# An expert's output in two rounded parts: the scatter product in one-pass form

## The reference

```
logits = x @ w_router                            # 256 x 8
top_logit, top_e = top_k(logits, 2)
gate = softmax(top_logit)
for each expert e, for the tokens routed to it:  # width 1024, hidden 3584
    y = (silu(x @ w_gate[e]) * (x @ w_up[e])) @ w_down[e]
    out[token] += gate[token, e] * y[token]
x = layer_norm(ALPHA * x + out)
```

## Time and profile before

| | |
|---|---|
| median of 3 runs | 1530.47 us (1529.55 to 1532.50) |
| profiled execution, first to last instruction | 1529.7 us |
| mean granted TensorE clock | 0.988 of full |
| TensorE busy (matmul) | 1478.0 us, 97% |
| VectorE busy | 1133.1 us, 74% |
| ScalarE busy | 966.3 us, 63% |
| read from memory | 427.87 MB |

### The profile page before, as it was taken

One profiled execution on the slowest core, in us unless ns is written; L12 is line 12 of the kernel. 1 busy time (PEld: TensorE's weight loads), 2 busy tenths in 40 slices (PEclk: granted clock), 3 DMA queues, 4 the chain that ended last, 5 costly groups with the idle time before them and its releaser, 6 DMA issues.

```text
span 1529.7 us, 20973 instructions
## 1 busy us (share of the span) xinstructions
PE 1478.0 (97%) x8040; PEld 1264.5 (83%) x8040; DVE 1133.1 (74%) x935; ACT 966.3 (63%) x910; POOL 6.2 (0%) x15
## 2 busy tenths in 40 slices
PE   8988999999988999999999999999999999999995
PEld 8987999989977788888888878888888888887883
DVE  4636444454546688888888888888888888888885
ACT  4644443355545677677677767767767767766774
POOL 1000000000000000000000000000000000000000
PEclk9999999999999999999999999999999999999998
DMA  9414555535044899799889889989989988998931
GB/s 369 148 63 167 191 186 179 189 136 185 37 193 184 323 376 377 308 369 371 340 339 373 344 334 379 369 302 375 378 322 355 370 340 337 375 371 309 377 137 57
DMA packets 59586, 429.63 MB, mean 281 GB/s; under 512 B 6720, under 2 KB 6736, under 8 KB 7568
## 3 DMA queue, kind: packets, MB, share of 16 engines
q1 hardware_dynamic: 58464, 423.65, 72.4%
q0 software_dynamic: 928, 5.02, 1.0%
q10 hardware_dynamic: 144, 0.27, 0.1%
HBM read 427.87 MB, written 1.05 MB: 280 GB/s over the span
## 4 chain that ended last, share of the span: by engine, by line
PE 91%; ACT 4%; DVE 3%; issue 1%; DMA 1%; SPq 0%; DVEq 0%; ACTq 0%
PE ps L397 27%; PE ps L399 27%; PE ps L398 27%; PE ps L684 2%; PE ps L671 2%; PE ps L693 2%; PE ps L404 1%; DVE wlo L1014 1%; ACT raw L822 1%; DMA raw<-w_dense 1%; DVE raw L1042 1%; PE ps L493 1%; ACT whi L760 1%; ACT biasb L796 1%; PE ps L549 1%
## 5 line engine op out<-in xcount | busy, mean ns | idle before, releaser
L1014 DVE TENSOR_TENSOR wlo<-raw,whi 128x2048 fp32r<-128x2048 f32 x402 | 920.8, 2291 | 242.3 <-ACT whi L760 242.0
L760 ACT ACTIVATE whi<-raw 128x2048 fp32r<-128x2048 f32 x402 | 770.4, 1918 | 313.3 <-PE ps L399 309.1
L397 PE MATMUL ps<-whi,xth 128*128 128x512 f32 (+1 forms) x1080 | 423.1, 392 | 7.5 <-ACT xth L775 6.5
L399 PE MATMUL ps<-whi,xtl 128*128 128x512 f32 (+1 forms) x1080 | 410.9, 380 | 0.0
L398 PE MATMUL ps<-wlo,xth 128*128 128x512 f32 (+1 forms) x1080 | 410.2, 380 | 0.0
L397 PEld LDWEIGHTS ps<-whi,xth 128*128 128x128 f32 x1080 | 204.3, 189 | 50.1 <-ACT xth L775 7.3
L398 PEld LDWEIGHTS ps<-wlo,xth 128*128 128x128 f32 x1080 | 204.5, 189 | 40.1 <-issue 3.8
L399 PEld LDWEIGHTS ps<-whi,xtl 128*128 128x128 f32 x1080 | 204.1, 189 | 39.5
L397 PE MATMUL ps<-whi,hth 128*128 128x512 f32 x528 | 206.4, 391 | 0.0
L399 PE MATMUL ps<-whi,htl 128*128 128x512 f32 x528 | 205.6, 389 | 0.0
L398 PE MATMUL ps<-wlo,hth 128*128 128x512 f32 x528 | 205.6, 389 | 0.0
(11 more groups left out here) (201 smaller groups left out, 800.5 us busy)
## 6 DMA issues: line engine op xcount, KB each, us to landing
raw<-w_moe SPq DMA_DIRECT2D x339, 1024.0 KB, 4.8
raw<-w_dense SPq DMA_DIRECT2D x63, 1024.0 KB, 4.8
raw<-vec_rows POOLq DMA_DIRECT2D x4, 1024.0 KB, 6.0
x<-x_in SPq DMA_DIRECT2D x2, 512.0 KB, 5.5
out<-x SPq DMA_DIRECT2D x2, 512.0 KB, 2.8
work<-bias_cst POOLq DMA_DIRECT2D x1, 576.0 KB, 8.7
con<-cst ACTq DMA_DIRECT2D x1, 262.0 KB, 4.7
work<-lam_rows POOLq DMA_DIRECT2D x1, 96.0 KB, 7.9
```

The costliest lines, as they stand in the source:

```text
L397: mm(o, lh, rh, start=start, stop=False)
L399: return mm(o, ll, rh, start=False, stop=stop)
L760: A(unit(whi, j), raw[:, slot * UNIT:(slot + 1) * UNIT], ACT.Copy).then_inc(hi_rdy, 1)
L1014: dve.tensor_tensor(unit(wlo, j), raw[:, slot * UNIT:(slot + 1) * UNIT], unit(whi, j).bitcast(F32), ALU.subtract).then_inc(lo_rdy, 1)
```

## The change

Between ScalarE's copy and the scatter, the expert's output is kept as a rounded half and a rest. ScalarE copies the two banks into the free columns 128 to 255 of `xth` (float32r), with a semaphore step for each bank. VectorE then subtracts this half from the banks and writes the rest into columns 128 to 255 of `xtl`; it does so at unit 41, behind the low part of the weights. `ohot_t` becomes a float32r tile of its own. Each of the four plain products of a scatter is replaced by two one-pass products that accumulate in the same bank, and the scatter waits for the rest (`yl_rdy`). At the start of the expert stage VectorE fills the rest with zeros. `y` is gone, `work` is smaller by 256 columns, and three small tables that lay there move.

```diff
-        work = sb("work", [P, 1536])
+        work = sb("work", [P, 1280])
+        ohot_t = sb("ohot_t", [P, TOK], F32R)
...
-        wr_raw = work[:, B_END:B_END + 64].rearrange("p (k n) -> p k n", n=8)
-        sub_g = work[:, B_END + 64:B_END + 192]
-        lam_in = work[:, B_END + 192:B_END + 384].rearrange("p (i n) -> p i n", n=DH)
+        wr_raw = extra[:, 5712:5776].rearrange("p (k n) -> p k n", n=8)
+        sub_g = work[:, B_END:B_END + 128]
+        lam_in = extra[:, 5520:5712].rearrange("p (i n) -> p i n", n=DH)
-        y = work[:, 0:1024]
-        ohot_t = work[:, 1280:1536]
+        def out_half(t, nn):
+            return t[:, 4 * nn:4 * nn + 4, P:TOK]
+
+        def out_bank(nn):
+            return ps[5 + nn][:, :].rearrange("p (k n) -> p k n", k=4)
...
             def scatter(n, tb):
                 if tb == 0:
-                    pe.wait_ge(ye_rdy, n + 1)
+                    pe.wait_ge(yl_rdy, n + 1)
                     pe.wait_ge(oht_rdy, n + 1)
                 for nn in range(2):
                     i = 2 * tb + nn
                     if tb == 1:
                         pe.wait_ge(sc_acc, n * 4 + (i - 1))
-                    mm(ps[7 if i % 2 == 0 else 4][:, :], ohot_t[:, tb * P:(tb + 1) * P],
-                       y[:, nn * 512:(nn + 1) * 512], start=True, stop=True).then_inc(sc_ps, 1)
+                    bank = ps[7 if i % 2 == 0 else 4]
+                    mm(bank[:, :], ohot_t[:, tb * P:(tb + 1) * P], out_half(xth, nn), start=True, stop=False)
+                    mm(bank[:, :], ohot_t[:, tb * P:(tb + 1) * P], out_half(xtl, nn),
+                       start=False, stop=True).then_inc(sc_ps, 1)
...
                     if j == PER_EXP - 1:
                         act.wait_ge(w_used, e * PER_EXP + (N_DENSE + j + 1))
                         for nn in range(2):
-                            r = A(y[:, nn * 512:(nn + 1) * 512], ps[5 + nn][:, :], ACT.Copy)
-                        r.then_inc(ye_rdy, 1)
+                            A(out_half(xth, nn), out_bank(nn), ACT.Copy).then_inc(ye_rdy, 1)
...
+            def expert_out_lo(n):
+                for nn in range(2):
+                    dve.wait_ge(ye_rdy, 2 * n + (nn + 2))
+                    r = dve.tensor_tensor(out_half(xtl, nn), out_bank(nn), out_half(xth, nn).bitcast(F32), ALU.subtract)
+                r.then_inc(yl_rdy, 1)
...
+                    if j == PER_EXP - 1:
+                        expert_out_lo(e)
             one_hot(0, 0)
+            dve.wait_ge(ye_rdy, 1)
+            dve.tensor_scalar(xtl[:, :, P:TOK], iota.unsqueeze(1).to_broadcast([P, 8, P]), 0.0, None,
+                              ALU.mult).then_inc(yl_rdy, 1)
             gathered(0)
```

More of the change, by code:

```diff
@@ L268, in trunk @@
         oht_rdy = sem("onehot_t_ready")
-        ye_rdy = sem("expert_out_ready")
+        ye_rdy = sem("expert_out_hi_ready")
+        yl_rdy = sem("expert_out_lo_ready")
         sc_ps = sem("scattered_in_psum")
@@ L952, in _ @@
             act.wait_ge(flag_rdy, 1)
-            A(y, iota.unsqueeze(1).to_broadcast([P, 8, P]), ACT.Copy, scale=0.0).then_inc(ye_rdy, 1)
-            A(ohot_t, con[:, 0:256], ACT.Copy, scale=0.0).then_inc(oht_rdy, 1)
+            A(xth[:, :, P:TOK], iota.unsqueeze(1).to_broadcast([P, 8, P]), ACT.Copy, scale=0.0).then_inc(ye_rdy, 1)
+            A(ohot_t[:, :], con[:, 0:256], ACT.Copy, scale=0.0).then_inc(oht_rdy, 1)
             def gathered(n):
@@ L968, in expert @@
                         act.wait_ge(oht_ps, e + 1)
-                        A(ohot_t, ps[7][:, 0:256], ACT.Copy).then_inc(oht_rdy, 1)
+                        A(ohot_t[:, :], ps[7][:, 0:256], ACT.Copy).then_inc(oht_rdy, 1)
                     if (what, half) == ("up", 1):
```

## The result

The changed kernel takes 1514.56 us (median of 5 runs, 1512.38 to 1517.77), the kernel before 1530.47 us in the same comparison. The ratio is 0.9914, 95% interval 0.9893 to 0.9934: faster by 0.7 to 1.1%. The median lies 0.9 us under the low end of the forecast's range; by the ratio, 0.9914 x 1530.47 = 1517.3 us, it lies inside. The profiled spans differ by more than either: 1529.7 - 1512.3 = 17.4 us, and a part of that is not the change's.

The account below looks back on a forecast made before the run. TensorE alone was taken to bound the expert stage. Scatter -12.96, stalls +3.2 and tail -1.4 make -11.2 us: span 1529.7 to 1518.5, 1519.3 us for the runs, range 1515.5 to 1524.0.

Parts of the forecast that it names:

- What bounds the kernel: Expert stage: TensorE alone bounds it, gather to gather 124.96 us; time taken from its stream comes off the run.
- The scatter call: Scatter on TensorE: four one-pass products, 0.907 us instead of 1.72; 0.81 us off per call, 12.96 us for 16 calls.
- rival of a dearer pass: Scatter products with moving operand in pieces: at 0.43 us per pass nothing gained, stalls remain, 1533.7 us; chance 0.06.
- The stall: Ahead of an expert's first scatter call: TensorE waits 0.45 us for the rest, 7 times, 3.2 us (1.5 to 4.2).
- What is late next: Vector engine's queue behind the subtractions: margin before the hidden transpose shrinks from 0.97 to 0.16 us; zero wait, bound 1.6 us.
- the second rival: Handovers: vector engine doesn't catch up, 1.29 us stay on the path at each of 7, +9.0 us, 1528.3 us; chance 0.07.
- Edits at no cost: ScalarE's strided copies, zero fill of the rest (at most 1.3 us, hidden in a 5.05 us wait) and moved tables cost nothing.
- The tail: Last scatter and accumulations after the loop: end at 1516.05 instead of 1517.46, 1.4 us off, bounds 0.5 and 2.0.
- the pause: TensorE's 3.38 us "issue" stop in the last scatter may move or go: 1515.9, or 1522.7 us with a second; chance 0.09.
- The sum: Whole kernel: -12.96 + 3.2 - 1.4 = -11.2 us, giving 1518.5 us for the span and 1519.3 for the runs.
- The transfers: Expert stage: weight transfers become the bound and all the gain comes back, about 1530.5 us; chance 0.03.
- the closer passes: Scatter on TensorE: a call's four products overlap at 131 ns each, 19.1 us gained instead of 12.96, 1513.2 us; chance 0.01.

Follow-up runs that it names:

- plain-product variant: Changed kernel with each bank's scatter as one plain fp32 product of the rounded half again, subtraction and wait kept, rest left out: 1531.37 us, ratio 1.0022.
- variant without the wait: Changed kernel with TensorE waiting only for ScalarE's copies, both products reading the rounded half, the rest still made but unread: 1513.19 us, ratio 0.9896.
- doubled subtractions: Changed kernel with two more subtractions of the same size, their result unread, ahead of the real two: 1522.41 us, ratio 0.9957.

## Why the prediction was right, point by point

**What bounds the kernel**: right. With two calls dearer by 1.62 us in all, the plain-product variant's experts each took 1.62 us longer than the changed kernel's.

**The scatter call**: right. 0.81 us a call was forecast; the first expert, which has no stall, shows 122.46 - 120.84 = 1.62 us for two, and the plain-product variant the same. The rival of a dearer pass is out: the four pieces stream at 0.23 us.

**The stall**: right in place and cause, a fifth too large. The forecast was 0.45 us; the timeline shows 0.37 and the variant without the wait 0.36, by 7 about 2.6 us instead of 3.2. The rest was late by 0.20 us (627.21 against 627.01; 0.21 forecast) and the second product by 0.11 more (0.10 forecast). The term that was off is the latency from the subtraction's end to the weight load. I took 0.14 us from the one restart at the first gather; here it is 627.27 - (625.93 + 1.28) = 0.06 us.

**What is late next**: right. The margin ahead of the hidden transpose was forecast at 0.16 us and is 0.15; no wait appeared there, nor at the second call. The sign that I gave for the second rival was too wide, though. I wrote that a chain through the low parts would make the prediction wrong, and the chain does pass through the low part of unit 2, because the subtractions stand behind it, as in my own working of the stall. The rival asked for 1.29 us per handover on top of the stall. It is ruled out by the seven waits being the only ones, by the vector engine waiting for ScalarE again at 633.20, and by the doubled subtractions, which cost 1.19 us per expert and no more.

**Edits at no cost**: right for the zero fill. It takes 0.69 us (from 491.57), behind it the vector engine still waits 4.45 us for the gather, and the first expert has the whole 1.62 us of two calls. That the moved tables cost nothing is not shown to better than the spread ahead of the first gather.

**The tail**: undersized, and outside its bounds of 0.5 to 2.0 us. Behind the pause the forecast was 1.4 us; between the pairs of traces it is 5.48 - 4.29 = 1.19 us, and 2.3 us for the second pair (the kernel before again, 1511.64 + 0.75 - 1505.79 = 6.60; the changed one again, 1500.19 + 1.61 - 1497.50 = 4.30). The two differ by the clock of the kernel before: in its first trace the granted clock was 1.00 from 1515 to 1517 us, while the last accumulations ran, in its second 0.50 until 1511; in both traces of the changed kernel it was 0.50 throughout, as the forecast had it. The whole tail gave 2.94 us, and (1524.6 - 1486.56) - (1514.0 - 1478.75) = 2.79 us in the second pair. Most of the excess in the first pair is the pause, 1.5 us shorter; this was a rival of mine, in a mild form, and it looks like chance, since the pause was 4.13 us in the repetition. The wait of the first product for the rest, of which I forecast none, cost nothing.

**The sum**: -9.8 us in the loop was forecast; 997.18 - 986.57 = 10.61 and 997.18 - 986.72 = 10.46 us less were measured, and the smaller stall is the difference. With the tail that makes 13.2 to 13.6 us against 11.2. Of the 2.2 us that the forecast missed, about 1.5 are the tail and 0.7 the stall. By the ratio the gain is 0.86% or 13.2 us, with 10.1 to 16.4 in the interval. The median went further, by 15.9 us; in the second comparison the medians are 1527.94 - 1515.91 = 12.0 us apart. What lies ahead of the first gather is a likely reason, though not a shown one, since only the profiled runs show that stage: one kernel differs there by 6.3 us from run to run, twice what the 0.2% allows for. My range made no room for that term, since I had one trace and no spread of a stage, so how near a single median falls is in part luck. One bound was added up wrong: -12.96 + 4.2 + 1.6 - 0.5 = -7.7 gives 1522.8 us, not 1522.0; the stated range covers it.

**The transfers and the closer passes**: out. Nothing was given back, and no pass was closer than 0.23 us.

## What to carry to other kernels

A plain fp32 product cost as much here as almost four one-pass products of the same size (0.86 us against 0.227). Where one operand is exact in the rounded form (here zeros and ones), two passes are enough. The split cost the vector engine 1.29 us per expert and ScalarE nothing more (1.06 us for two copies, as before). Before adding a step on a second engine, ask where in that engine's queue it lands: put behind the weights' low part it cost 0.36 us per expert, put ahead of it, with ScalarE's copies moved forward too, nothing. To compare two traces, use distances inside the loop: they repeated to 0.02 us per expert, while the start of the loop moved by 6 us in unchanged code.

## What was not expected of the hardware

In the two traces of the unchanged kernel the stretch from 440 to 445 us ran once at a granted clock of 0.50 (1.2 GHz) and once at 1.00 (2.4 GHz), and the first gather came at 495.69 and 489.38 us. That stretch accounts for 87.56 - 84.69 = 2.87 us of these 6.3. The other 3.44 were there before it (a block of the chain at 408.13 against 404.69). The granted clock in 345 to 350 us, 0.75 in the first trace and 1.00 in the second, goes with 1.49 of them (from a rounding at 325.19 or 323.24 us to the block at 401.24 or 397.80); the rest isn't explained.

TensorE stops at the start of the tail's scatter, for nothing shown, in every trace, and not by the same time in two runs of one kernel (1.97 and 3.37 us in the changed one). In eight traces it stops between the first two records, for 2 to 3.4 us; in that of the variant without the wait it stands from the first weight load (1491.09) to the first product (1495.44).
